# A sixth block in each up stage of a tuned Trainium2 kernel, with twice only one plain pair between two blocks

## The reference, cut to what matters

```python
def conv_ffn(xn, w_up, conv_w, conv_b, w_down):     # w_up: 1024 x 5632, conv over 3 tokens
    h = causal_dwconv(xn @ w_up, conv_w) + conv_b
    gate, val = h[..., :FFN_DIM], h[..., FFN_DIM:]  # FFN_DIM = 2816 = 22 tiles of 128
    return (jax.nn.silu(gate) * val) @ w_down
```

## Time and profile before

| | |
|---|---|
| time, median of 3 runs (lowest to highest) | 1739.49 us (1735.94 to 1739.52) |
| the profiled execution: its own time | 1736.82 us |
| the profiled execution: span of the trace | 1734.9 us |
| mean granted TensorE clock | 0.999 |
| PE busy in the span | 1712.4 us (99%) |
| DVE, ACT busy | 1314.2 us (76%), 943.2 us (54%) |
| first up stage, f = 2 to 21 | 387.75 to 605.99 us |

### The profile page before, as it was taken

One profiled execution on the slowest core, in us unless ns is written; L12 is line 12 of the kernel. 1 busy time (PEld: TensorE's weight loads), 2 busy tenths in 40 slices (PEclk: granted clock), 3 DMA queues, 4 the chain that ended last, 5 costly groups with the idle time before them and its releaser, 6 DMA issues.

```text
span 1734.9 us, 26654 instructions
## 1 busy us (share of the span) xinstructions
PE 1712.4 (99%) x9926; PEld 1383.8 (80%) x9926; DVE 1314.2 (76%) x2262; ACT 943.2 (54%) x1577; POOL 67.4 (4%) x105
## 2 busy tenths in 40 slices
PE   9999999999999999999999999999999999999998
PEld 6777777778888888888887788888888766678987
DVE  7788888569888795767776689887956577677875
ACT  6665666455444462567777554444534466754442
POOL 2000000000000000000000000000000000001100
PEclk9999999999999999999999999999999999999999
DMA  5522122123443322333332234533232312235531
GB/s 188 179 84 74 63 72 62 49 86 104 146 127 103 129 96 84 107 116 109 103 105 68 75 114 134 140 91 140 69 111 75 109 37 73 92 114 130 159 113 62
DMA packets 60838, 177.52 MB, mean 102 GB/s; under 512 B 7489, under 2 KB 12884, under 8 KB 60720
## 3 DMA queue, kind: packets, MB, share of 16 engines
q1 hardware_dynamic: 50928, 152.46, 26.1%
q0 software_dynamic: 9360, 23.38, 6.1%
q10 hardware_dynamic: 432, 0.07, 0.0%
HBM read 169.26 MB, written 6.63 MB: 101 GB/s over the span
## 4 chain that ended last, share of the span: by engine, by line
PE 88%; DVE 5%; ACT 3%; issue 2%; DMA 1%; POOL 0%; SPq 0%; DVEq 0%; ACTq 0%
PE acc L1109 9%; PE acc L1083 9%; PE acc L1084 8%; PE acc L1085 8%; PE pa L1452 3%; PE pbc L1454 3%; PE pbc L1452 3%; PE pa L1454 3%; PE pbc L1453 3%; PE pa L1453 3%; PE pa L1439 2%; PE pa L1438 2%; PE pa L1437 1%; PE acc L1480 1%; PE acc L1479 1%
## 5 line engine op out<-in xcount | busy, mean ns | idle before, releaser
L1083 PE MATMUL acc<-xhi,wsplit 128*128 128x512 f32 x448 | 189.3, 422 | 1.0 <-DVE at_vs L3303 1.0
L2139 ACT ACTIVATE wsplit<-wraw 128x512 fp32r<-128x512 f32 (+1 forms) x130 | 105.0, 825 | 153.0 <-PE pbc L1454 53.6
L2599 DVE TENSOR_TENSOR wsplit<-wraw,wsplit 128x1024 fp32r<-128x1024 f32 (+1 forms) x122 | 151.9, 1248 | 44.7 <-ACT wsplit L1821 43.9
L1085 PE MATMUL acc<-xhi,wsplit 128*128 128x512 f32 x448 | 177.4, 396 | 0.0
L1084 PE MATMUL acc<-xlo,wsplit 128*128 128x512 f32 x448 | 177.4, 396 | 0.0
L1821 ACT ACTIVATE wsplit<-wraw 128x1024 fp32r<-128x1024 f32 (+1 forms) x125 | 133.7, 1073 | 76.7 <-PE acc L1085 52.1
L1109 PE MATMUL acc<-xhi,wsplit 128*128 128x512 f32 x464 | 158.2, 413 | 0.1
L3006 DVE TENSOR_TENSOR wsplit<-wraw,wsplit 128x512 fp32r<-128x512 f32 (+1 forms) x130 | 119.6, 934 | 31.7 <-ACT wsplit L2139 31.6
L1083 PEld LDWEIGHTS acc<-xhi,wsplit 128*128 128x128 f32 x448 | 84.3, 188 | 33.5 <-issue 13.8
L1085 PEld LDWEIGHTS acc<-xhi,wsplit 128*128 128x128 f32 x448 | 84.3, 188 | 20.2
L2236 ACT ACTIVATE wsplit<-wraw 128x512 fp32r<-128x512 f32 (+1 forms) x90 | 52.2, 600 | 86.7 <-PE pa L1439 25.2
(11 more groups left out here) (645 smaller groups left out, 4613.2 us busy)
## 6 DMA issues: line engine op xcount, KB each, us to landing
wraw<-w SPq DMA_DIRECT2D x215, 512.0 KB, 3.7
wraw<-w SPq DMA_DIRECT2D x75, 256.0 KB, 3.3
wraw<-w POOLq DMA_DIRECT2D x34, 256.0 KB, 5.5
wraw<-w SPq DMA_DIRECT2D x8, 704.0 KB, 6.0
wraw<-w SPq DMA_DIRECT2D x24, 192.0 KB, 2.4
bias_dram<-ext_dram POOLq DMA_DIRECT2D x1, 4096.0 KB, 20.8
bias<-bias_dram POOLq DMA_DIRECT2D x16, 256.0 KB, 3.0
at_ks<-at_ks SPq DMA_DIRECT2D x16, 256.0 KB, 2.9
```

The lines of the kernel that those rows point to most:

```text
L1083: mm(out, whi[:, k, :], a[:, x_at + k, :], start=(k == first), stop=False)
L1085: m = mm(out, wlo[:, k, :], a[:, x_at + k, :], start=False, stop=(k == last))
L2139: A(unit_split(u, 0), unit_raw(u), ACT.Copy).then_inc(ev("block_act"), 1)
L2599: tt_(split(s, i, j, 1), raw(s, j), split(s, i, j, 0).bitcast(F32), ALU.subtract).then_inc(w_lo_ready, 1)
```

## The change

The list of blocks goes from five to six, 6, 9, 11, 14, 17, 19 in place of 6, 9, 12, 15, 18. Between 9 and 11, and between 17 and 19, lies only one plain pair. For these two "close" blocks (UP_CLOSE) DVE makes s2 in the gate half of the pair ahead (behind ev 0) in place of the value half of the pair before that, and s4 in its value half (behind ev 1) in place of the gate half. The ring gets two pads, at the gates of 10 and 18. The loops of SP, POOL, ACT and PE are not edited; they follow UP_BLOCKS.

```diff
-UP_BLOCKS = (6, 9, 12, 15, 18)
+UP_BLOCKS = (6, 9, 11, 14, 17, 19)
+UP_CLOSE = tuple(f for f in UP_BLOCKS if f - 2 in UP_BLOCKS)
-UP_PADS = ((19, 'gate'),)
+UP_PADS = ((10, 'gate'), (18, 'gate'))
@@ up_counts, plain pair
-            dve += [("ev", f, 0)] + lows((f, "gate")) + [("tap", f, 0), ("conv", f, 0)]
+            dve += [("ev", f, 0)]
+            if f + 1 in UP_CLOSE:
+                dve += [("s2", f + 1)]
+            dve += lows((f, "gate")) + [("tap", f, 0), ("conv", f, 0)]
             act += his((f, "gate")) + [("newest", f, 0)]
-            if f + 1 in UP_BLOCKS:
+            if f + 1 in UP_BLOCKS and f + 1 not in UP_CLOSE:
                 dve += [("s4", f + 1)]
...
             if f + 2 in UP_BLOCKS:
                 dve += [("s2", f + 2)]
+            if f + 1 in UP_CLOSE:
+                dve += [("s4", f + 1)]
@@ ffn of the vector engine, pair(f)
                     tt_(tmp[:, 0, :], pa[:, 0, :], rstd[:], ALU.mult).then_inc(steps, 1)
+                    if f + 1 in UP_CLOSE:
+                        sum_low(f + 1)
                     lows_after((f, "gate"))
...
-                    if f + 1 in UP_BLOCKS:
+                    if f + 1 in UP_BLOCKS and f + 1 not in UP_CLOSE:
                         sum_high(f + 1)
...
                     if f + 2 in UP_BLOCKS:
                         sum_low(f + 2)
+                    if f + 1 in UP_CLOSE:
+                        sum_high(f + 1)
                     lows_after((f, "value"))
```

## The result

| | before | after |
|---|---|---|
| median | 1737.99 us (1735.94 to 1739.52, 4 runs) | 1761.17 us (1760.87 to 1761.45, 4 runs) |
| ratio | | 1.0138, 95% interval 1.0125 to 1.0151 |
| profiled execution | 1736.82 us, span 1734.9 | 1761.45 us, span 1759.2 |
| mean granted clock | 0.999 | 0.992 |

The change makes the kernel 23.2 us slower by the medians, 1.4% by the recorded ratio. Over 21 further executions the median of the kernel before is 1736.92 us, and against that one the loss is 24.2 us. The result is inside the recorded range (1746 to 1764) and of the forecast sign, 7 us above the forecast of 1754.

What follows compares the result with a forecast made beforehand. PE's streaming and any wait of it bound the kernel. Two close blocks in two stages, 4 x (3.9 + 0.5) = +17.6 us, less 2.76, gave +14.8 on 1739.49: 1754 us; range for 8 in 10, 1746 to 1764.

Steps and rivals of the forecast that it cites:

- the signs that would have shown it wrong: Gate 10 landing before 473.3, waits at pairs 10 and 18 under 1 us, or PE waiting inside blocks 11 and 19.
- the second rival: Clock falls in the stalls at pairs 10 and 18: 2.5 us a stall; 1759 for half, 1764 for all; chance 18%.
- second waits: PE waits behind each close block, at pairs 12 and 20, for the gate's low part: 0.5 us, bounds 0 and 2.3.
- The saving: One pair turned into a block saves 1.38 us in each up stage, 2.76 us in two.
- The moved loads: On SP, block 11's bases go ahead of gate 10 and value 10, behind a22's low part; gate 10 issued 6.6 us later.
- The first wait: PE stalls at the start of pairs 10 and 18, in both stages: 3.9 us each, bounds 2.6 and 5.1.
- The walk: Step-by-step timing of DVE and PE from D through block 11: gate 12's low ends D + 22.85, PE begins D + 23.1.
- D: Start of DVE's low part of gate 10: 472.24 before, forecast 477.7 after.
- The sums: POOL's accumulating loads for block 11 done by 484.4 at the latest, wanted by s2 at 487.9; costed at nothing.
- DVE's load: A block and one pair take 19.9 us on DVE against 21.1 on PE; costed at nothing.
- the end of the stage: Two plain pairs after block 19, 22.5 us of PE against 15.0 of DVE, absorb some 4 us lag; costed at nothing.
- the pads: Pair 10's slots free a11 to s1 one tile later, with 5.62 us for 2.6 us of lows; costed at nothing.

Runs made afterwards that it cites:

- the run that kept the clock up: Changed kernel with 16 more matmuls of resident data on PE ahead of its wait for the gate's low part at pairs 10 and 18; 1756.96 us, ratio 1.0115.
- the run with SP's wait kept: Changed kernel with gate and value loaded ahead of the close block's bases, but still behind SP's wait for a22's low part; 1741.52 us, ratio 1.0024.
- the run with gate and value first: Changed kernel with SP loading the bases of close blocks 11 and 19 one turn later, behind the pair's gate and value; 1734.75 us, ratio 0.9986.
- seven blocks: Changed kernel with close blocks' bases loaded behind gate and value, blocks 6, 8, 11, 13, 16, 18, 20 and six pads; 1735.79 us, ratio 0.9997.
- the one with the bases early: Kernel before, its five blocks kept, with the bases of blocks 9, 12, 15 and 18 loaded one turn earlier; 1799.01 us, ratio 1.0359.

## Why the prediction was right, and where its sizes were off

The mechanism was right, and none of the signs that would have shown it wrong came. The forecast of the time rests on stalls at full clock, and there it was not right: without the clock's part the measured terms would give about 1752 us. That 1761 still lies inside the range is owed to its upper end, which was drawn wide enough for the second rival, and to second waits that did not come.

*What bounds the kernel.* Right. PE's time was the kernel's, and each wait came through in full.

*The saving.* Sized 2.76 us. With the waits gone the spans of the stages give 2.4, the times 2.2.

*The moved loads.* Right, shown from both sides: mended in the changed kernel, the whole loss goes; put into the kernel before, it comes.

*The first wait.* Forecast 3.9 us, bounds 2.6 to 5.1; measured 4.00, 4.84, 3.92 and 4.53. The landing was sized a little short: 4.6 us from the issue of the gate, where the four needed 4.9 to 6.0. At the first of them the forecast had 6.3 us from the first base's issue to the gate's split, the trace 6.7. The rule of the Trainium skill, "DMA: Bandwidth & Descriptors", section "Queues, rings and completion order", that each engine takes a ring's descriptors in order, fits these loads: behind the bases the gates need 4.9 to 6.0 us from their issue, ahead of them 3.5 to 3.7. It is not shown by them, as loads that only share the engines would slow each other as well.

*The second wait.* Forecast 0.5 us at four places; none in the changed kernel. In the run that kept the clock up it is there, about 0.35 us in three places and 0.7 in the fourth, and in the run with SP's wait kept, about 0.3 us each time. The walk itself was good: block 11's low of gate 12 was put at D + 21.6, and in the run with gate and value first it starts at 493.38, D (471.86) + 21.5.

*The clock.* This is the term that was mis-sized. The forecast left it out of its sum and gave it 18% as a rival; it came behind all four waits, at 2.1 us each (2.5 had been estimated), 8.4 us, and that rival's price for the fall in all four stalls was 1764. The row for it was read, a clock at the lower level after 2.8 us without a matmul, with an expected wait of 3.9 us beside it; the argument against it was the full stream of matmuls ahead of the wait, and that did not keep the clock up: a block of 9.86 to 9.97 us without a gap stood ahead of each. 14.8 - 2.0 (second waits) + 1.7 (first waits, 17.3 for 15.6) + 8.4 is 22.9 us. The medians differ by 23.2; the two profiled executions, from which the terms are read, by 24.3 in their spans.

*What was costed at nothing.* The sums, DVE's load, the end of the stage and the pads together cost no more than the 0.4 us by which the run with gate and value first stays short of its saving. With seven blocks the end of the stage does begin to cost.

## What to carry to other kernels

Where a schedule is derived from a list, an edit of the list also moves steps in queues that the diff does not show; go through each in-order queue, DMA issue above all, and ask what now stands in front of what. A prefetch that waits for its buffer should not stand ahead of a load that is due sooner and could go at once. And price a wait of TensorE at its length plus what the clock costs behind it: here 4.3 us of waiting cost 6.4.

## What the runs showed of the hardware that was not expected

The clock fell after shorter waits than thought. A wait of 2.10 us was followed by 3.50 us at 0.51. One of 2.00 us in the delta stage of another run (SP's wait kept) stood behind 6.90 us of full work, and 0.35 us after PE had begun again the clock was at 0.50 for 3.41 us:

```profile
70.00:76.90 6.90, 6.90 (x38) 5.04 (x36) 3.88 (x8) 5.06 (x8) 0.07 (x1) 1.00 0.73 175
76.90:78.92 2.02, 0.02 (x1) 0.00 (x1) 1.46 (x6) 0.28 (x1) 0.00 (x0) 1.00 0.00 0
78.92:79.27 0.35, 0.35 (x3) 0.35 (x4) 0.35 (x1) 0.35 (x1) 0.00 (x0) 1.00 0.00 0
79.27:82.68 3.41, 3.41 (x13) 2.85 (x12) 1.07 (x2) 1.49 (x3) 0.00 (x0) 0.50 0.39 101
```

So a fall can begin in the wait, as at pair 10 of the changed kernel (0.87 on average in the stretch of the wait), or behind it.

Shorter waits left it at 1.00 in every run. The longest of them were 1.33 us and 1.57 us in an up stage, behind a full stream, and 1.55 to 1.81 us some 13 us from the start of four runs. The second of these and the last, from the run with SP's wait kept and the one with the bases early:

```profile
1126.30 0.47 PE L1461 MATMUL pa<-xhi,wsplit 128*128 128x512 f32 x1 [1.57 <-DVE tmp L3125]
```

```profile
13.35 0.50 PE L1142 MATMUL acc<-xhi,wg_hi 128*128 128x512 f32 x1 [1.81 <-DVE xlo L2624]
```

A wait of 4.8 us that was filled for 3.8 us left it at 1.00 too. No wait between 1.81 and 2.00 us was seen, and whether the length of the wait alone decides was not tested.
